# S5 inputs on TensorE: real and imaginary parts of two tiles in four row groups, with a swapped copy of the input

## The chip, the cores and the metric

One core of one Trainium2 chip runs the whole kernel. The metric is the device time of one launch in microseconds (us); less is better. TensorE (PE) multiplies, VectorE (DVE), ScalarE (ACT) and GpSimd (POOL) work elementwise, SyncE (SP) only issues DMAs. The engines run side by side, each in its own program order, and meet at semaphores.

## The reference, cut to what matters

A decoder block on x of 256 tokens by 2048 channels, float32. An RMSNorm and one wide projection `hn @ w_in` feed two token mixers, a Mamba-2 (SSD) mixer and an S5 mixer; their results are gated and merged, and a convolutional gated MLP follows. The change touches the S5 mixer alone:

```python
ug = u.reshape(b, seqlen, 64, 16)                     # 64 groups of 16 channels
bu = einsum("gpc,blgc->blgp", b_bar, ug)              # complex, 64 states a group
_, states = associative_scan(_lin_rec, (a_el, bu))    # over the 256 tokens
y = einsum("gcp,blgp->blgc", cmat, states).real + d_skip * ug
y = gelu(y); val, gate = split(y @ w_glu); return val * sigmoid(gate)
```

So for every group of 16 input channels, B (64 states by 16 channels, a real and an imaginary part) is multiplied with u over all tokens.

## The kernel before, in words

All activations lie channel-major: 128 channels on the partitions, the 256 tokens along the free axis. A large product is cut into units: 512 input by 256 output channels, 512 KB of weights. For each unit SP loads `raw` (L250) into a ring of 4 slots, ScalarE rounds it to a high half `whi` (L432), VectorE subtracts to get the low half `wlo` (L809), and TensorE runs 16 matmuls (L1363 on `whi`, 512 columns; L1365 on `wlo`, 256 columns). ScalarE reuses a slot only when TensorE has used it (`unit_used`). 588 units follow one another in the phases dt, u, zx, bc, gate, proj, glu, out, up and down.

In the phases zx (6 turns) and bc (2 turns) every turn has 16 units, four for each r of 0 to 3, and carries one block of the S5 mixer (blk 0 to 7): 8 groups of 16 channels, thus 128 input channels and 4 tiles of 128 states. Tile r takes the 32 input channels of rows 32r to 32r + 31. The steps of a block:

- `load_b` (L267 to 271, GpSimd DMAs) brings B into `bz`: rows 32r + 16g, both parts, block-diagonal; 8 DMAs a block.
- `ubs` is the block's 128 channels of u (`ub`). ScalarE makes the first (L593), GpSimd the later ones (L392), once the second drive of the block before is done.
- `s5_drive(blk, r)` (L1397 to 1408, TensorE) comes after the first unit of r = 0 and of r = 2 and computes tiles r and r + 1: 4 float32 matmuls of 32 rows by 128 columns on 256 tokens. The float32 matmuls appear in the trace as two records (passes) each. Tile r goes to PSUM bank 4 or 6, real part in the lower half and imaginary part in the upper half.
- VectorE turns the result back by the angle tables (`s5_turn_back` L956, `s5_inputs` L965), scans it (L976) and turns it on (L981, L982); `s5_products(blk)` (L1410 to 1420, TensorE), 16 float32 matmuls in four column groups, comes in the next turn and writes `YS5`, lower half of bank 5. `fill_c` (GpSimd, L380) prepares C for it.

GpSimd's order is written out by hand: constants, the loads of B for block 0, a long chain of small operations for the S5 parameters (L299 to L374, with the write of the decay rows, L354, in its midst) that ends in `cfold`, then `fill_c(0)`, then the loop over the blocks, then `load_decay` (L277) for the gate phase, which fills `dec` for VectorE's scan (L1104). VectorE copies the transposed time steps `DTT` (bank 5) to `dtt` at L1059, in the first turn, and TensorE waits for that in r = 1, q = 2 (L1433 and L1434).

A turn of VectorE has for every r: a `wlo`, the group's sums (L815), the turn back, a `wlo`, the causal convolution (L995), the scan, two further `wlo`, the turn on and the fractions of the angles (L953). In bc the convolution comes with every r, in zx with every second.

Of the kernel before, what the change touches and what calls it, by code (L numbers as in the profile page):

```python
# [24 lines left out]
F32, F32R, I32 = mybir.dt.float32, mybir.dt.float32r, mybir.dt.int32  # L25
ALU, ACTF = mybir.AluOpType, mybir.ActivationFunctionType
ds = bass.ds

P = 128
L = 256  # L30
# [64 lines left out]
def build_program(nc, a, out):  # L95
    ctx = ExitStack()
    with ctx:
# [4 lines left out]
        def at(name, shape, dt, off):  # L102
            size = 4 * math.prod(shape[1:])
            assert off + size <= room, (name, off, size, room)
            return nc.alloc_sbuf_tensor_at(name, shape, dt, offset=base + off)
# [14 lines left out]
        ub = at("ub", [P, 8, L], F32, 168 * K)  # L120
# [11 lines left out]
        bz = at("bz", [P, 2, P], F32, 138 * K)  # L132
        sx = at("sx", [P, 2, L], F32, 139 * K)
        ubs = at("ubs", [P, L], F32, 141 * K)
# [12 lines left out]
        W = 176 * K  # L147
# [7 lines left out]
        dtt = at("dtt", [P, 2, HEADS], F32, W + 20480)  # L155
        dtw = at("dtw", [P, 7, L], F32, W)
        ncz = at("ncz", [P, 4, 32], F32, W + 20864)

        C = W + 21 * K
        hw = at("hw", [P, 2, L], F32, 189 * K)  # L160
# [11 lines left out]
        scr = nc.dram_tensor("decay_rows", (HEADS, L), F32).ap()  # L172

        psum = ctx.enter_context(nc.psum_tensor("psum", [P, 8, 512], F32))
        BU = [psum[:, b, :].rearrange("p (c n) -> p c n", c=2) for b in (4, 6)]
        YS5 = psum[:, 5, 0:L]
        CB, XP = psum[:, 4, 0:ML], [psum[:, 5, 0:ML], psum[:, 6, 0:ML]]
        YY = [psum[:, 7, 0:L], psum[:, 7, L:2 * L], psum[:, 4, 0:L]]
# [1 line left out]
        DTT = psum[:, 5, 0:2 * HEADS].rearrange("p (s h) -> p s h", s=2)  # L180

        def sem(name):
# [3 lines left out]
        x_in, w_in, b_in = [[sem(f"{n}{k}") for k in range(4)] for n in ("x_in", "w_in", "b_in")]  # L186
# [13 lines left out]
        dtp_in, dt_in, dt_exp, dt_row, dt_T, dt_v = map(sem, ("dtp_in", "dt_in", "dt_exp", "dt_row", "dt_T", "dt_v"))  # L200

        s5_square, s5_inv, s5p_ready, u_ready, iota_ready, angm_ready = map(
            sem, ("s5_square", "s5_inv", "s5p_ready", "u_ready", "iota_ready", "angm_ready"))
        ubs_ready, ncz_ready, bu_used, modulus_ready = map(sem, ("ubs_ready", "ncz_ready", "bu_used", "modulus_ready"))
        th_ready, sincos, bu_ready, ang_ready, tab_ready, x5_ready, y5_ready, cz_ready, y5_out, y5_gelu, y5_hi, y5_lo = map(
            sem, ("th_ready", "sincos", "bu_ready", "ang_ready", "tab_ready", "x5_ready", "y5_ready", "cz_ready",
                  "y5_out", "y5_gelu", "y5_hi", "y5_lo"))
# [52 lines left out]
        def _(pool):  # L260
# [4 lines left out]

            def load_b(blk, r):

                for g in range(2):
                    pool.dma_start(bz[32 * r + 16 * g:32 * r + 16 * g + 16, :, 64 * g:64 * g + 64],
                                   a["s5_b"][ds(blk * 8 + (2 * r + g), 1), :, :, :]  # L270
                                   .rearrange("o c k n -> (o c) k n")).then_inc(b_in[r], 16)

            def load_decay(g, half):

                rows = scr[ds(g * HPG + half * HALF, HALF), :]
                for lo, off in ((0, 0), (P, L)):
                    pool.dma_start(dec[half][:, :, off:off + L - lo],  # L277
                                   rows[:, lo:L].rearrange("(o h) n -> o h n", o=1).to_broadcast([P, HALF, L - lo])
                                   ).then_inc(dec_in[half], 16)
# [96 lines left out]
            def fill_c(blk):  # L376

                for g in range(2):
# [2 lines left out]
                                  .rearrange("p c r n -> p r c n")).then_inc(cz_ready, 1)  # L381
                    pool.wait_ge(cz_ready, blk * 2 + (g + 1))

            pool.wait_ge(s5p_ready, 1)
            fill_c(0)
            pool.wait_ge(u_ready, 4)
            with pool.Fori(0, 7) as i:
                pool.wait_ge(bu_ready, i * 2 + 1)
                load_b(i + 1, 0)
                load_b(i + 1, 1)  # L390
                pool.wait_ge(bu_ready, i * 2 + 2)
                G.tensor_copy(ubs[:, :], ub[:, ds(i + 1, 1), :].rearrange("p o n -> p (o n)")).then_inc(ubs_ready, 1)  # L392
                load_b(i + 1, 2)
                load_b(i + 1, 3)
                pool.wait_ge(y5_ready, i + 1)
                fill_c(i + 1)
            pool.wait_ge(scr_w, 16)
            pool.wait_ge(dt_v, 1)
            load_decay(0, 0)
            pool.wait_ge(y5_ready, 8)  # L400
            load_decay(0, 1)
# [399 lines left out]
        def _(dve):  # L801
            step = Tally(dve, dve_step)
            V = nc.vector
# [146 lines left out]
            def s5_fractions(count):  # L950

                dve.wait_ge(angm_ready, count)
                V.scalar_tensor_tensor(ang[:, :, :], angm[:, :, :], MAGIC, ang[:, :, :], ALU.subtract,  # L953
                                       ALU.subtract).then_inc(ang_ready, 1)
# [85 lines left out]
            def mixer_turn(name, i, blk, prev):  # L1040

                _, per, quads, u0, g0 = phase(name)
                start = prev[0] == "u"
                for r in range(per):
                    def lo(j):
                        split_lo(u0 + r * quads + j + RING, i * (per * quads))
                    before = (name, i, r - 1) if r else prev
                    last = name == "bc" and i == 1 and r == per - 1
                    tile = blk * 4 + r
                    lo(0)  # L1050
                    group_sums(*before)
                    s5_turn_back(r, blk * 4 + (r + 1), blk * 2 + (r // 2 + 1), start and r == 0)
                    s5_inputs()
                    lo(1)
                    group_conv(*before)
                    if r == 0 and start:

                        dve.wait_ge(dt_T, 1)
                        V.tensor_copy(dtt[:, :, :], DTT).then_inc(dt_v, 1)  # L1059
                    if r == 1 and start:  # L1060
                        dve.wait_ge(scr_w, 16)
                    s5_scan(tile)
                    lo(2)
                    cpad_free(*before)
                    if r == 0 and not start:
                        s5_out(blk - 1)
                    s5_turn_on(r)
                    if not last:
                        s5_fractions(blk * 4 + (r + 2))
                    lo(3)  # L1070

            s5_fractions(1)
            dve.wait_ge(modulus_ready, 1)
            mixer_turn("zx", 0, 0, ("u", 0, 3))
            with dve.Fori(1, 6) as i:
# [266 lines left out]
        def _(pe):  # L1342
            mm = nc.tensor.matmul

            def unit(name, r, q, act, i=0):

                groups, quads, per = PHASES[name]
                n, g = UNIT0[name] + r * quads + q, GROUP0[name] + r
                pe.wait_ge(lo_ready, i * (per * quads) + (n + 1))
                if q == 0 and g + (i * per if isinstance(i, int) else 0) >= 2:  # L1350

                    pe.wait_ge(sum_ready, i * per + (g - 1))
                s, b = n % RING, 2 * (g % 2)
                for k in range(4):
                    row = 4 * q + k
                    x = act[:, row + (KT if name == "down" and row >= KT else 0), :]
                    first, last = q == 0 and k == 0, q == quads - 1 and k == 3
                    tiles = range(1 if name == "dt" else 2)

                    def cols(t):  # L1360
                        return slice(k * L + t * P, k * L + t * P + P)
                    for t in tiles:
                        mm(psum[:, b + t, :], whi[:, s, cols(t)], x, start=first, stop=False)  # L1363
                    for t in tiles:
                        ins = mm(psum[:, b + t, L:2 * L], wlo[:, s, cols(t)], x[:, 0:L], start=False, stop=last)  # L1365
                ins.then_inc(unit_used, 1)
# [7 lines left out]
            for k in range(KT):  # L1374
                c = k // 4
# [21 lines left out]
            def s5_drive(blk, r, first=False):  # L1397

                pe.wait_ge(ubs_ready, blk + 1)
                if not (first and r == 0):  # L1400
                    pe.wait_ge(bu_used, blk * 4 + r)
                for j in (r, r + 1):
                    pe.wait_ge(b_in[j], blk * 32 + 32)
                for k in range(2):
                    for j in (r, r + 1):
                        rows = slice(32 * j, 32 * j + 32)
                        ins = mm(BU[j % 2][:, k, :], bz[rows, k, :], ubs[rows, :], start=True, stop=True)
                ins.then_inc(bu_ready, 1)

            def s5_products(blk):  # L1410
# [11 lines left out]
            def mixer_turn(name, i, blk, prev):  # L1422

                for r in range(4):
                    for q in range(4):
                        if prev is None and r == 0:
                            pe.wait_ge(vlo_ready, q + 1)
                        unit(name, r, q, act16, i)
                        if q == 0 and r % 2 == 0:
                            s5_drive(blk, r, prev is None)  # L1430
                        if q == 1 and r == 0 and prev is not None:
                            s5_products(prev)
                        if prev is None and r == 1 and q == 2:  # L1433
                            pe.wait_ge(dt_v, 1)  # L1434

            mixer_turn("zx", 0, 0, None)
            with pe.Fori(1, 6) as i:
# [158 lines left out]
```

## Time and profile before

| | us |
|---|---|
| median of 3 runs (1750.8 to 1751.63) | 1751.62 |
| the profiled execution's own time | 1750.85 |
| its span, first to last instruction | 1749.2 |
| TensorE busy in the span | 1717.9 |
| VectorE busy | 1368.6 |
| ScalarE busy | 961.6 |
| GpSimd busy | 166.8 |

The mean granted TensorE clock is 0.998 of full speed. Busy times overlap between engines; TensorE's are modelled from pipelined matmuls, so that a busy TensorE need not be at its peak. The span is 1.65 us shorter than the execution's own time.

### The profile page before, as it was taken

To read this page: it belongs to the slowest core of one execution; us is meant where nothing else is said; L and a number is where in the kernel's file an instruction comes from. 1 tells how busy PE (TensorE), PEld (TensorE's weight loads), DVE (VectorE), ACT (ScalarE), POOL (GpSimd) and SP (SyncE) were. 2 spreads that over 40 slices of the span, in tenths; PEclk is the share of its full clock that TensorE was granted. 3 is DMA by queue.
4 is the path that set the end of the run, shared out by engine and by line. 5 is a ranking of instruction groups with operands and counts; after the bars stand their busy time and mean duration, and the time that the engine had idled before them with its cause. 6 is when DMAs were issued, how large, how long until landed. Compare 5 with 4: busy or idle time off the path is not lost.

```text
span 1749.2 us, 30494 instructions
## 1 busy us (share of the span) xinstructions
PE 1717.9 (98%) x10094; PEld 1483.0 (85%) x10094; DVE 1368.6 (78%) x1889; ACT 961.6 (55%) x1233; POOL 166.8 (10%) x240
## 2 busy tenths in 40 slices
PE   7999999999999999999999999999999999999997
PEld 6888888888788888888888888888888888888886
DVE  6999999999989898545886678888888888645544
ACT  6566666566656666645665554444444444444442
POOL 7920111101011110000001100000000000000000
PEclk9999999999999999999999999999999999999999
DMA  7555455545565655555566655555555555565652
GB/s 246 187 183 184 167 169 170 181 158 186 179 198 173 220 186 192 185 189 192 187 223 192 191 192 189 186 188 185 187 184 190 186 187 190 194 194 190 191 186 105
DMA packets 91415, 326.25 MB, mean 187 GB/s; under 512 B 11344, under 2 KB 12368, under 8 KB 91232
## 3 DMA queue, kind: packets, MB, share of 16 engines
q1 hardware_dynamic: 86320, 313.42, 54.3%
q0 software_dynamic: 5040, 12.11, 2.5%
q8 instruction: 32, 0.52, 0.1%
q14 instruction: 23, 0.19, 0.0%
HBM read 323.35 MB, written 2.15 MB: 186 GB/s over the span
## 4 chain that ended last, share of the span: by engine, by line
PE 62%; DVE 6%; issue 3%; ACT 2%; DVEq 1%; ACTq 0%
PE psum L1363 41%; PE psum L1365 20%; DVE dec L1104 2%; DVE wlo L809 1%; ACT whi L432 1%; ACT L444 1%; DVE zx L1162 0%; DVE zx L1165 0%; DVE gates L815 0%; DVE bc L995 0%; DVE zx L1085 0%; PE psum L1453 0%; DVE vn L1338 0%; DVE zx L827 0%; ACT rs L444 0%
## 5 line engine op out<-in xcount | busy, mean ns | idle before, releaser
L809 DVE TENSOR_TENSOR wlo<-raw,whi 128x1024 fp32r<-128x1024 f32 x588 | 720.5, 1230 | 321.2 <-ACT whi L432 319.6
L432 ACT ACTIVATE whi<-raw 128x1024 fp32r<-128x1024 f32 x588 | 619.1, 1057 | 442.3 <-PE psum L1365 433.5
L1363 PE MATMUL psum<-act,whi 128*128 128x512 f32 x1792 | 566.8, 398 | 0.0
L1363 PE MATMUL psum<-nw,whi 128*128 128x512 f32 x1552 | 488.7, 396 | 4.4 <-DVE wlo L809 4.2
L1365 PEld LDWEIGHTS psum<-act,wlo 128*128 128x128 f32 x1792 | 336.6, 188 | 79.6
L1365 PE MATMUL psum<-act,wlo 128*128 128x256 f32 x1792 | 352.2, 278 | 0.0
L1365 PEld LDWEIGHTS psum<-nw,wlo 128*128 128x128 f32 x1552 | 291.6, 188 | 68.2
L1365 PE MATMUL psum<-nw,wlo 128*128 128x256 f32 x1552 | 306.2, 278 | 0.0
L1363 PEld LDWEIGHTS psum<-act,whi 128*128 128x128 f32 x1792 | 272.7, 189 | 10.0 <-issue 6.6
L1363 PEld LDWEIGHTS psum<-nw,whi 128*128 128x128 f32 x1552 | 236.9, 189 | 6.4 <-issue 3.9
L1363 PE MATMUL psum<-ff,whi 128*128 128x512 f32 x704 | 221.1, 395 | 0.0
L1365 PEld LDWEIGHTS psum<-ff,wlo 128*128 128x128 f32 x704 | 132.2, 188 | 31.3
L1365 PE MATMUL psum<-ff,wlo 128*128 128x256 f32 x704 | 138.3, 278 | 0.0
L1363 PE MATMUL psum<-y_hl,whi 128*128 128x512 f32 x384 | 120.8, 396 | 0.0
L1363 PEld LDWEIGHTS psum<-ff,whi 128*128 128x128 f32 x704 | 107.2, 189 | 0.0
L760 ACT ACTIVATE tsum<-tsum 128x256 f32<-128x256 f32 x44 | 18.5, 419 | 131.2 <-DVE tsum L995 131.2
L1365 PEld LDWEIGHTS psum<-y_hl,wlo 128*128 128x128 f32 x384 | 72.1, 188 | 17.0
L440 ACT ACTIVATE hsum<-psum 128x512 f32<-128x512 f32 (+1 forms) x137 | 79.1, 577 | 10.0 <-PE psum L1365 10.0
L1363 PE MATMUL psum<-yb_hl,whi 128*128 128x512 f32 x256 | 80.4, 395 | 0.0
L1365 PE MATMUL psum<-y_hl,wlo 128*128 128x256 f32 x384 | 75.4, 278 | 0.0
L995 DVE SCALAR_TENSOR_TENSOR tsum<-cpad,parm,tsum 128x256 f32<-128x256 f32 x176 | 73.5, 480 | 0.1
L1363 PEld LDWEIGHTS psum<-y_hl,whi 128*128 128x128 f32 x384 | 58.5, 189 | 0.1
(186 smaller groups left out, 1389.0 us busy)
## 6 DMA issues: line engine op xcount, KB each, us to landing
raw<-in_w_up SPq DMA_DIRECT2D x176, 512.0 KB, 4.3
raw<-in_w_zx SPq DMA_DIRECT2D x96, 512.0 KB, 3.3
raw<-in_w_down SPq DMA_DIRECT2D x88, 512.0 KB, 4.2
raw<-in_w_gate SPq DMA_DIRECT2D x64, 512.0 KB, 3.8
raw<-in_w_proj SPq DMA_DIRECT2D x48, 512.0 KB, 3.3
raw<-in_w_bc SPq DMA_DIRECT2D x32, 512.0 KB, 3.2
raw<-in_w_glu SPq DMA_DIRECT2D x32, 512.0 KB, 3.2
raw<-in_w_out SPq DMA_DIRECT2D x32, 512.0 KB, 4.0
```

The lines of the kernel that those rows point to most:

```text
L432: fn(whi[:, s, :], raw[:, s, :], ACTF.Copy).then_inc(hi_ready, 1)
L440: fn(hsum[:, tiles, :], sums(g, 1)[:, tiles, :], ACTF.Copy).then_inc(hsum_ready, 1)
L444: step.done(fn(rs[:, :], NS, ACTF.Ln, bias=EPS, scale=1.0 / count))
L760: fn(tsum[:, 0, :], tsum[:, 0, :], ACTF.Silu).then_inc(silu2_done, 1)
L809: V.tensor_tensor(wlo[:, s, :], raw[:, s, :], whi[:, s, :], ALU.subtract).then_inc(lo_ready, 1)
L995: ins = V.scalar_tensor_tensor(to[t], src, col(w, q * taps + k), to[t], ALU.mult, ALU.add)
L1104: ins = V.tensor_tensor_scan(dec[half][:, k, :], dec[half][:, k, :], mask[:, :], 0.0, ALU.add, ALU.mult)
L1363: mm(psum[:, b + t, :], whi[:, s, cols(t)], x, start=first, stop=False)
L1365: ins = mm(psum[:, b + t, L:2 * L], wlo[:, s, cols(t)], x[:, 0:L], start=False, stop=last)
```

## The change

B's imaginary part is loaded 64 rows away from its real part (row group r ^ 2), from the same input. A second copy of u, `ubx`, has its halves of 64 rows swapped, so that these channels stand there too. The drive multiplies the real parts of tiles r and r + 1 in row groups r and r + 1, and the imaginary parts in the two others. Every one of the four products has a PSUM bank of its own: tile 0 or 2 in the lower halves of banks 6 and 7, tile 1 or 3 in the upper halves of banks 4 and 5. `load_b` issues 16 DMAs a block instead of 8, of half the size; `swap_u` issues 2 more. `ubx` lies where `dtw` and `dec` lie at other times, so `load_decay(0, 0)` waits for the last drive. The copy of `DTT` out of bank 5 moves ahead of the first turn, and TensorE's wait for it ahead of the first drive.

```diff
+        ubx = at("ubx", [P, L], F32, W)
...
-        BU = [psum[:, b, :].rearrange("p (c n) -> p c n", c=2) for b in (4, 6)]
+        BU = [psum[:, 6:8, 0:L], psum[:, 4:6, L:2 * L]]
...
             def load_b(blk, r):
 
-                for g in range(2):
-                    pool.dma_start(bz[32 * r + 16 * g:32 * r + 16 * g + 16, :, 64 * g:64 * g + 64],
-                                   a["s5_b"][ds(blk * 8 + (2 * r + g), 1), :, :, :]
-                                   .rearrange("o c k n -> (o c) k n")).then_inc(b_in[r], 16)
+                for k, at_r in ((0, r), (1, r ^ 2)):
+                    for g in range(2):
+                        row = 32 * at_r + 16 * g
+                        pool.dma_start(bz[row:row + 16, k, 64 * g:64 * g + 64],
+                                       a["s5_b"][ds(blk * 8 + (2 * r + g), 1), :, k, :]
+                                       .rearrange("o c n -> (o c) n")).then_inc(b_in[r], 16)
+
+            def swap_u(blk):
+
+                for to, frm in ((0, 64), (64, 0)):
+                    pool.dma_start(ubx[to:to + 64, :], ub[frm:frm + 64, ds(blk, 1), :]
+                                   .rearrange("p o n -> p (o n)")).then_inc(ubx_in, 16)
...
+            pool.wait_ge(u_ready, 1)
+            swap_u(0)
             pool.wait_ge(s5p_ready, 1)
             fill_c(0)
             pool.wait_ge(u_ready, 4)
...
                 pool.wait_ge(bu_ready, i * 2 + 2)
                 G.tensor_copy(ubs[:, :], ub[:, ds(i + 1, 1), :].rearrange("p o n -> p (o n)")).then_inc(ubs_ready, 1)
+                swap_u(i + 1)
                 load_b(i + 1, 2)
...
             pool.wait_ge(dt_v, 1)
+            pool.wait_ge(bu_ready, 16)
             load_decay(0, 0)
...
-                    if r == 0 and start:
-
-                        dve.wait_ge(dt_T, 1)
-                        V.tensor_copy(dtt[:, :, :], DTT).then_inc(dt_v, 1)
...
             s5_fractions(1)
+            dve.wait_ge(dt_T, 1)
+            V.tensor_copy(dtt[:, :, :], DTT).then_inc(dt_v, 1)
             dve.wait_ge(modulus_ready, 1)
...
                 for j in (r, r + 1):
-                    pe.wait_ge(b_in[j], blk * 32 + 32)
-                for k in range(2):
+                    pe.wait_ge(b_in[j], blk * 64 + 64)
+                pe.wait_ge(ubx_in, blk * 32 + 32)
+                for k, u in enumerate((ubs, ubx)):
                     for j in (r, r + 1):
-                        rows = slice(32 * j, 32 * j + 32)
-                        ins = mm(BU[j % 2][:, k, :], bz[rows, k, :], ubs[rows, :], start=True, stop=True)
+                        rows = slice(32 * (j ^ 2 * k), 32 * (j ^ 2 * k) + 32)
+                        ins = mm(BU[j % 2][:, k, :], bz[rows, k, :], u[rows, :], start=True, stop=True)
...
                         unit(name, r, q, act16, i)
+                        if prev is None and r == 0 and q == 0:
+                            pe.wait_ge(dt_v, 1)
                         if q == 0 and r % 2 == 0:
                             s5_drive(blk, r, prev is None)
...
-                        if prev is None and r == 1 and q == 2:
-                            pe.wait_ge(dt_v, 1)
```

## Rows read from the trace of the kernel before

**Rows 1.** Busy time, share of the span and instructions of each engine.

```profile
PE 1717.9 (98%) x10094; PEld 1483.0 (85%) x10094; DVE 1368.6 (78%) x1889; ACT 961.6 (55%) x1233; POOL 166.8 (10%) x240
```

**Rows 2.** Waits (us, times, longest): VectorE 123-369; timeline 380-394; TensorE's waits 386-492.

```profile
DVE wlo L809 <- ACT whi L432: 12.9, 23, 1.0
...
383.10 1.23 DVE L809 TENSOR_TENSOR wlo<-raw,whi 128x1024 fp32r<-128x1024 f32 x1 [1.01 <-ACT whi L432]
...
PE psum L1469 <- DVE ub L1004: 2.3, 1, 2.3
```

**Rows 3.** TensorE timeline (start, us) at two drives; the drive's line as a whole.

```profile
74.40 1.13 PE L1407 MATMUL psum<-ubs,bz 32*128 32x256 f32 x8
75.47 0.73 PE L1363 MATMUL psum<-act,whi 128*128 128x512 f32 x2
...
367.37 1.13 PE L1407 MATMUL psum<-ubs,bz 32*128 32x256 f32 x8
...
L1407 PE MATMUL psum<-ubs,bz x128: 374/374/478, 74.4 to 442.9; 32*128 32x256 f32 x128
```

**Rows 4.** TensorE timeline: full-array float32 passes, and the S5 products.

```profile
12.75 2.54 PE L1378 MATMUL psum<-xsq,ones 128*128 128x256 f32 x11
...
174.75 1.50 PE L1419 MATMUL psum<-st,cz 128*32 128x256 f32 x24
176.07 0.61 PE L1419 MATMUL psum<-st,ncz 128*32 128x256 f32 x8
```

**Rows 5.** GpSimd timeline: the end of the S5 parameters.

```profile
17.40 4.71 POOL L316 CAST iota<-iotai 128x256 f32<-128x256 int32 x1 [7.14 <-DMA craw<-in_s_c]
...
71.66 0.63 POOL L354 DMA_DIRECT2D decay_rows<-dtw  x1 [0.29 <-POOL s5p L309]
...
77.91 2.32 POOL L309 TENSOR_TENSOR ctmp<-craw,s5p 128x512 f32<-128x512 f32 x2
...
81.76 3.39 POOL L309 TENSOR_TENSOR ctmp<-craw,s5p 128x512 f32<-128x512 f32 x2
...
87.07 1.85 POOL L374 TENSOR_TENSOR cfold<-ctmp 128x512 f32<-128x512 f32 x1
```

**Rows 6.** VectorE timeline around the first drive.

```profile
74.80 0.73 DVE L953 SCALAR_TENSOR_TENSOR ang<-angm,ang 128x512 f32<-128x512 f32 x1
...
80.44 2.32 DVE L809 TENSOR_TENSOR wlo<-raw,whi 128x1024 fp32r<-128x1024 f32 x1
```

**Rows 7.** GpSimd's DMAs: landing of `bz` (L269), and issues with KB and landing.

```profile
DMA to landing us min/median/max: 1.7/2.7/3.8
...
decay_rows<-dtw POOLq DMA_DIRECT2D x1, 48.0 KB, 2.1
...
dec<-decay_rows POOLq DMA_DIRECT2D x16, 192.0 KB, 6.4
```

**Rows 8.** Stretches: length, busy (x) PE PEld DVE ACT POOL, PEclk, DMA, GB/s; PE timeline.

```profile
6.40:9.90 3.50, 3.50 (x8) 2.83 (x9) 2.54 (x6) 2.00 (x2) 3.17 (x9) 1.00 1.02 370
9.90:13.30 3.40, 3.40 (x17) 2.94 (x16) 3.40 (x9) 3.09 (x4) 0.36 (x2) 1.00 1.02 413
...
1737.59 1.13 PE L1520 MATMUL psum<-sq,ones 128*128 128x256 f32 x4 [2.00 <-ACT sq L749]
...
1740.80:1749.00 8.20, 0.00 (x0) 0.00 (x0) 4.63 (x4) 0.16 (x1) 0.00 (x0) 0.50 0.64 256
```

**Rows 9.** GpSimd and VectorE timelines in the mixer phase, and the first decay scan.

```profile
197.63 1.37 POOL L392 COPY ubs<-ub 128x256 f32 x1 [16.44 <-PE psum L1407]
198.94 2.00 POOL L269 DMA_DIRECT2D bz<-in_s_b  x4
...
198.66 0.68 DVE L815 TENSOR_TENSOR cpad<-psum,hsum 128x512 f32<-128x512 f32 x1
199.26 0.68 DVE L962 TENSOR_TENSOR rot<-psum,tab 128x512 f32<-128x512 f32 x1
...
471.98 2.64 DVE L1104 TENSOR_TENSOR_SCAN dec<-dec,mask 128x384 f32<-128x384 f32 x3
```

More of the change, by code:

```diff
@@ L203, in build_program @@
             sem, ("s5_square", "s5_inv", "s5p_ready", "u_ready", "iota_ready", "angm_ready"))
-        ubs_ready, ncz_ready, bu_used, modulus_ready = map(sem, ("ubs_ready", "ncz_ready", "bu_used", "modulus_ready"))
+        ubs_ready, ncz_ready, bu_used, modulus_ready, ubx_in = map(
+            sem, ("ubs_ready", "ncz_ready", "bu_used", "modulus_ready", "ubx_in"))
         th_ready, sincos, bu_ready, ang_ready, tab_ready, x5_ready, y5_ready, cz_ready, y5_out, y5_gelu, y5_hi, y5_lo = map(
```

## The prediction

> **What bounds the kernel now.** I read the busy times, then the waits, and last the order of time at the edited places. TensorE is busy 98% of the span [rows 1]. Over five turns of the Mamba/S5 mixer phase VectorE waits 12.9 us in 23 pieces [rows 2], always for the high halves that ScalarE makes, and those wait for TensorE to free a slot: 2.6 us of idle in a turn, in a stretch of 246 us that is five turns of 49.2. So TensorE sets the pace there. That ends at 383.10, VectorE's last wait [rows 2]. From 386 to 492 us VectorE waits for nothing (the view of its waits is empty), and TensorE in turn waits for it, 2.3 us in one piece [rows 2]. Two prices follow. A microsecond that TensorE loses before 383 us is a microsecond of the whole, since every weight unit behind it comes through a ring of four. A microsecond that it saves counts only before 383 us; one saved later is waited away.
>
> **What four row groups save.** A drive is 8 records: 4 float32 matmuls, each in two passes. Before, the first drive runs from 74.40 to the next unit's start at 75.47, 1.07 us; all 16 have the same record lengths [rows 3]. How long is one slot of 256 columns? Eleven full-array passes take 2.54 us, at most 0.231 each [rows 4]. The S5 products, in four column groups, put 24 passes between 174.75 and 176.07; four at a time that is 6 slots of 0.22 [rows 4]. So the drive now has 4 slots of 0.22 (two row groups side by side, re after im) and 0.19 of filling and draining. Four row groups with a bank each would leave 2 slots: 1.07 - 0.44 = 0.63. No row shows four row groups; bounds are no overlap beyond two (0 saved) and the four-wide pattern of the products (0.44 saved). I take 0.44, since the products show four-wide column groups at work and the drives show two row groups. Thirteen of the 16 drives start before 383 us (the 13th at 367.37 [rows 3]). 13 x 0.44 = 5.7 us saved; all 16 would be 7.0.
>
> **What the first swapped copy costs.** This is the largest term. Before, the first drive needs only `ubs`, made by ScalarE, and runs at 74.40 [rows 3]. Now TensorE also waits for `ubx`, and `swap_u(0)` stands on GpSimd behind its whole S5 parameter arithmetic. GpSimd finishes the last of it, `cfold`, at 87.07 + 1.85 = 88.92 [rows 5]. TensorE is an in-order engine: behind the waiting drive are all units of the phase; VectorE and ScalarE may only fill the ring, then stop.
> When does the copy land? VectorE will be idle from about 78 us, and the two engines slow each other: the pair of 128x512 products at 77.91 takes 1.16 each, the same pair at 81.76 takes 1.70 each, and beside them VectorE's 1.2 us subtraction takes 2.32 [rows 5, 6]. If the seven operations from 77.91 on all take 1.16 and 0.09 between them, they end at 77.91 + 7 x 1.16 + 6 x 0.09 = 86.6; at the latest at 88.9 as before. The issue: 0.3 us ahead, as before the write of the decay rows, and 0.6 for the first of two transfers (0.50 to 0.63 [rows 5, 9]). Landing: no row has an SBUF-to-SBUF transfer; `bz` lands in 1.7 to 3.8 us, the 48 KB write of decay rows in 2.1 [rows 7]; I take 2.1, the nearest in row length. 86.6 + 0.3 + 0.6 + 2.1 = 89.6, a stall of 15.2 us. Bounds: 86.6 + 0.5 + 1.7 = 88.8 (14.4) and 88.9 + 0.3 + 0.6 + 3.8 = 93.6 (19.2).
> The Trainium skill, "SBUF — State Buffer", explains that VectorE and GpSimd share one port pair by an exclusive lock; the pairs above agree. The skill's "DMA: Bandwidth & Descriptors", Anatomy of one DMA, gives 2.0 us plus the bytes at 436 GB/s for a GpSimd transfer, an estimate of 2.15 us for these 64 KB; with it the stall would be the same.
>
> **What the idle costs in clock.** At the kernel's start TensorE does 8 records in 3.50 us, then 17 of the same kind in 3.40 [rows 8]: for the first 3.5 us after idling it goes at half pace, that of the 1.2 GHz level, though the clock column, which has no entry so early, prints 1.00. At the end, its last record over by 1737.59 + 1.13 = 1738.7, it is granted 0.50, the lower level, from before 1740.8 [rows 8]. A stall of 15 us must bring that back: 3.5 us at half speed lose 1.7. Bounds: 0 if the clock stays, 3.5 if it needs twice as long.
> The Trainium skill, "TensorE: Matmul & The Clock Gate", Part 1, says that idling halves the clock and sustained work restores it; had I left the rule and these rows out, the sum would be 1.7 lower.
>
> **The rest, at nothing.**
> - GpSimd's DMAs. At the start 8 more issues of 0.5 us are 4 us, inside GpSimd's 7.14 us of idle before 17.40 [rows 5]. In a turn 8 more loads and 2 copies are 5 us; the copy goes out behind the drive of r = 2 and is wanted by the next r = 0 drive, about half a turn or 24 us later, of which the `ubs` copy ahead of it takes 1.37 [rows 9], the two issues 1 and the landing 2.1. If that cover were gone TensorE would wait for it once a turn. The issues don't slow VectorE: beside four of them at 198.94 its operations take the same 0.68 as elsewhere [rows 9].
> - VectorE reading two banks: it does so now in `add_halves`, 0.68 us for 128x512 at 198.66, the same as the rotation's 0.68 from one bank at 199.26 [rows 9].
> - The move of `dtt`. VectorE makes the copy (0.24 us) after 74.80 + 0.7 [rows 6], so about 75.7; `dt_T` is long there. TensorE now waits for it ahead of the first drive, 1.4 us behind where it would start. That lies inside the stall; without the stall it costs 1.4 us. It no longer waits in r = 1.
> - `load_decay(0, 0)` now waits for the last drive, which is over by 444 us (last record started 442.9 [rows 3]); its two issues and 6.4 us to land [rows 7] make it about 452; the scan wants it at 471.98 [rows 9]. Behind it on GpSimd is only the second half, which waits for the products of the last turn anyway.
>
> **Sum.** The profiled execution took 1750.85 us. +15.2 + 1.7 - 5.7 = +11.2, so 1762.1. The median of the runs, 1751.62, is 0.77 above it: 1762.8.
>
> **Rivals.**
> 1. The four groups do not run together (the change doesn't do what it says): nothing saved, 1762.8 + 5.7 = 1768.5. For it: no row has four row groups. Against it: two run side by side, and four column groups do. 0.10.
> 2. Faster. The swapped copy isn't late, so no stall and no clock loss: 1751.6 - 5.7 = 1745.9. Its place is GpSimd's order: the copy would have to be issued before 71.5 us, so the arithmetic to end 15 us earlier, or the hardware to run the transfer ahead of it. Below a stall of 4 us the sign turns (4.0 + 1.7 = 5.7). Against it: each of these operations stands in order and in its own row. 0.03.
> 3. GpSimd's extra issues hold VectorE: ten of 0.5 us a turn are 5 us, against 2.6 - 0.9 = 1.7 us idle left, so 3.4 lost in each of 7 turns: 1762.8 + 24 = 1787. Against it, the 0.68 beside the issues. 0.03. The Trainium skill's "SBUF — State Buffer" warns of descriptor writing locked out by VectorE; as that delays GpSimd rather than VectorE, it would only use up the cover of some 19 us.
> 4. No measurable change, by the stall being shorter than any bound: 0.02.
>
> **How the numbers follow.** The forecast has 0.82. About 0.2%, 3.5 us, is what a measurement can tell from no change. The forecast's own bounds are 14.4 + 0 - 7.0 = +7.4 and 19.2 + 3.5 - 5.7 = +17.0: 1759 to 1768.6. Taking in rival 1 gives 1759 to 1769. Slower 0.95, same 0.02, faster 0.03.
>
> **What would show it.** Right: TensorE idle for about 15 us before the first drive, released by the landing of `ubx`; a granted clock of 0.5 beside it and matmuls at double pitch for some 3.5 us; in all later drives 8 records and 0.63 us to the next unit; turns of 48.3 us instead of 49.2; a TensorE wait near the end of the phase grown from 2.3 to about 3.6 us; GpSimd's `cfold` done near 86.6. Wrong: later drives waiting for `ubx` or `bz`; drives still of 1.07 us; or the first drive at 74.4, which would void the largest term.

## The result and the profile after

The changed kernel takes 1762.99 us (median of 6 runs, 1762.44 to 1763.46) against 1751.62 before (1750.80 to 1752.53): ratio 1.0064, 95% interval 1.0054 to 1.0073. It is slower by 11.4 us. The profiled execution took 1762.64 us with a span of 1761.0.

The span and the busy times of the changed kernel, as in [rows 1]:

```profile
span 1761.0 us, 30707 instructions
PE 1717.2 (98%) x10094; PEld 1482.2 (84%) x10094; DVE 1366.8 (78%) x1889; ACT 961.4 (55%) x1233; POOL 195.4 (11%) x320
```

TensorE's two longest waits of the mixer phase, from the view of the waits (us in total, times, longest):

```profile
PE psum L1420 <- DMA ubx<-ub: 11.8, 1, 11.8
...
PE psum L1482 <- DVE ub L1018: 2.6, 1, 2.6
```

No engine has more instructions, GpSimd excepted (80 more, all DMA issues). The time is in one wait. The timeline of TensorE at the first drive, as in [rows 3]:

```profile
88.91 0.80 PE L1420 MATMUL psum<-ubs,bz 32*128 32x256 f32 x2 [11.81 <-DMA ubx<-ub]
88.93 0.80 PE L1420 MATMUL psum<-ubx,bz 32*128 32x256 f32 x2
89.47 0.66 PE L1420 MATMUL psum<-ubs,bz 32*128 32x256 f32 x2
89.52 0.64 PE L1420 MATMUL psum<-ubx,bz 32*128 32x256 f32 x2
90.08 1.22 PE L1375 MATMUL psum<-act,whi 128*128 128x512 f32 x2
```

and GpSimd's timeline ahead of it, as in [rows 5]:

```profile
72.98 3.93 POOL L319 TENSOR_TENSOR ctmp<-craw,s5p 128x512 f32<-128x512 f32 x2
...
79.19 3.38 POOL L319 TENSOR_TENSOR ctmp<-craw,s5p 128x512 f32<-128x512 f32 x2
...
85.09 1.26 POOL L384 TENSOR_TENSOR cfold<-ctmp 128x512 f32<-128x512 f32 x1
86.30 1.15 POOL L280 DMA_DIRECT2D ubx<-ub  x2
```

The first copy goes out when `cfold` is done, at 86.3, its second transfer lands at 88.8 and TensorE starts at 88.9 instead of 74.4. The two transfers from issue to landing, in the view of that line from 80 to 90 us:

```profile
DMA to landing us min/median/max: 1.9/1.9/2.0
```

The pair of matmuls at 90.08 takes 1.22 us instead of 0.73: half clock. The stretches show it (columns as in [rows 8]):

```profile
81.10:94.80 13.70, 5.89 (x22) 4.59 (x23) 5.20 (x8) 0.63 (x1) 6.67 (x8) 0.50 0.20 61
94.80:100.00 5.20, 5.20 (x32) 4.53 (x32) 3.55 (x5) 3.55 (x5) 0.69 (x2) 1.00 0.22 66
```

The granted clock is 0.50 from 81.1 to 94.8 us, of which 5.9 us lie behind the start of the first drive. That is the 1.2 GHz level; TensorE had idled since 88.91 - 11.81 = 77.1. (It was at this level in two other stretches, 19.7 to 26.5 and 490.7 to 494.1 us, of which more below.) Two later drives, in the same view of TensorE:

```profile
163.05 0.48 PE L1420 MATMUL psum<-ubs,bz 32*128 32x256 f32 x2
163.06 0.48 PE L1420 MATMUL psum<-ubx,bz 32*128 32x256 f32 x2
163.37 0.38 PE L1420 MATMUL psum<-ubs,bz 32*128 32x256 f32 x2
163.38 0.38 PE L1420 MATMUL psum<-ubx,bz 32*128 32x256 f32 x2
163.69 0.73 PE L1375 MATMUL psum<-act,whi 128*128 128x512 f32 x2
...
211.38 0.48 PE L1420 MATMUL psum<-ubs,bz 32*128 32x256 f32 x2
```

Four records start together, four more 0.32 us later, and the next unit follows 0.64 us after the start, where it took 1.06 to 1.07. A turn, between these two drives of the same r, is 48.33 us (49.2 before).

The shift of the k-th matmul of the weight units (k from 0) against the kernel before, worked out from both traces as the start in the run less the start in the kernel before, in us, shows where each run gains and loses:

| k-th matmul, its start before | after | e3 | e4 | e6 | e9 | e11 | e2 | e7 |
|---|---|---|---|---|---|---|---|---|
| 0, 17.4 | +0.9 | 0.0 | +1.3 | +0.5 | +0.6 | +0.4 | +1.0 | +0.5 |
| 290, 72.0 | +2.6 | +0.2 | +2.5 | +1.9 | +1.2 | +1.1 | +2.8 | +0.6 |
| 320, 78.4 | +16.7 | +18.1 | +2.5 | +16.5 | +17.1 | +13.7 | +2.6 | +0.2 |
| 440, 100.5 | +16.3 | +18.1 | +2.5 | +16.1 | +18.4 | +13.3 | +2.2 | +0.6 |
| 2000, 399.7 | +11.3 | +18.1 | +2.5 | +12.0 | +13.3 | +8.2 | -2.9 | -4.5 |
| 2300, 456.6 | +10.4 | +18.1 | +2.5 | +12.0 | +12.5 | +7.4 | -3.7 | -5.3 |
| 2500, 503.2 | +11.7 | +18.1 | +2.5 | +11.5 | +13.8 | +8.7 | +0.2 | -4.0 |
| the last, 1734.4 | +11.7 | +18.1 | +2.5 | +11.6 | +13.8 | +8.7 | +0.2 | -4.0 |

In the changed kernel the loss is all there at 78.4 us; 0.42 us come back at every drive; and from 456.6 to 503.2 some 1.3 us are lost again, as much as the last three drives had saved (3 x 0.42).

### The profile page after: what moved, and what is told of

It reads as the page before. It is cut to its first block, busy times and chain, and to the rows that moved or that the text cites. A ratio compares the mean times of both kernels' runs of the same rounds, so it can differ in the third digit from the quotient of the medians.

```text
span 1761.0 us, 30707 instructions
## 1 busy us (share of the span) xinstructions
PE 1717.2 (98%) x10094; PEld 1482.2 (84%) x10094; DVE 1366.8 (78%) x1889; ACT 961.4 (55%) x1233; POOL 195.4 (11%) x320
## 3 DMA queue, kind: packets, MB, share of 16 engines
HBM read 323.35 MB, written 2.15 MB: 185 GB/s over the span
## 4 chain that ended last, share of the span: by engine, by line
PE 62%; DVE 6%; issue 3%; ACT 2%; DVEq 0%; ACTq 0%
PE psum L1375 41%; PE psum L1377 20%; DVE dec L1116 2%; DVE wlo L823 1%; ACT whi L446 1%; ACT L458 0%; DVE zx L1174 0%; DVE zx L1177 0%; DVE gates L829 0%; DVE bc L1009 0%; PE psum L1466 0%; DVE zx L1097 0%; DVE vn L1350 0%; DVE zx L841 0%; ACT rs L458 0%
## 5 line engine op out<-in xcount | busy, mean ns | idle before, releaser
L1375 PEld LDWEIGHTS psum<-act,whi 128*128 128x128 f32 x1792 | 273.9, 189 | 11.3 <-issue 7.3
L1377 PEld LDWEIGHTS psum<-y_hl,wlo 128*128 128x128 f32 x384 | 72.1, 188 | 17.1
L273 POOL DMA_DIRECT2D bz<-in_s_b x128 | 62.4, 489 | 28.0 <-DVE ub L915 11.2
```

The source lines that it names most:

```text
L273: pool.dma_start(bz[row:row + 16, k, 64 * g:64 * g + 64], a["s5_b"][ds(blk * 8 + (2 * r + g), 1), :, k, :] .rearrange("o c n -> (o c) n")) ...
```

## The experiments

Each ran beside the kernel before on its chip; medians of that kernel were 1751.7 to 1751.9 us.

**e3_wait_only: the wait without the four groups.** The kernel before (two row groups, loads of B whole, `DTT` copied where it was), with `ubx` made and waited for and not read. `load_decay(0, 0)` waits for the last drive as in the changed kernel.

```diff
+            pool.wait_ge(u_ready, 1)
+            swap_u(0)
             pool.wait_ge(s5p_ready, 1)
...
                 for j in (r, r + 1):
                     pe.wait_ge(b_in[j], blk * 32 + 32)
+                pe.wait_ge(ubx_in, blk * 32 + 32)
```

> The kernel before, with the swapped copies made and waited for but not read: two row groups as before, loads of B as before. Theory: it has the whole stall and clock loss and no saving, 1763.0 + 5.5 = 1768.5 us, drives of 1.06 us, a wait of 12 us or more ahead of the first. Rival (the wait is made by the moved copy of DTT or by the split loads): 1751.6 us.

Measured: 1768.31 us (ratio 1.0091, 1.0076 to 1.0107). TensorE's wait, from the view of its waits:

```profile
PE psum L1420 <- DMA ubx<-ub: 14.7, 1, 14.7
```

The wait alone, with its clock, costs 16.4 us. In the medians the changed kernel is 5.3 us faster than this one, where 13 x 0.42 = 5.5 was expected of four row groups. The two profiled executions differ by 6.4 us: 0.5 because the first copy landed later here (the drive starts at 89.41), 0.84 at the first drive, which ran at half clock in both (2.01 us here, 1.17 in the changed kernel), and 12 x 0.42 = 5.0 at the twelve drives behind it. In the table e3 stays at +18.1 from 78.4 us to the end; nothing later takes it back.

**e4_loads_only: the doubled loads without the rest.** The kernel before, each load of B as two DMAs.

```diff
-                for g in range(2):
-                    pool.dma_start(bz[32 * r + 16 * g:32 * r + 16 * g + 16, :, 64 * g:64 * g + 64],
+                for k in range(2):
+                    for g in range(2):
+                        row = 32 * r + 16 * g
+                        pool.dma_start(bz[row:row + 16, k, 64 * g:64 * g + 64],
...
-                    pe.wait_ge(b_in[j], blk * 32 + 32)
+                    pe.wait_ge(b_in[j], blk * 64 + 64)
```

> The kernel before, with each load of B split in two (16 DMAs a block instead of 8), nothing else. Theory: hidden, 1751.6 us within 0.5, TensorE's first drive at 74.4. Rival (the 2.7 us by which the changed kernel is late even ahead of its first drive, with the clock halved from 19.7 to 26.5 us, come from the eight further loads at the start): 1754 us, the first drive at 77.

Measured: 1752.40 us (1.0002, 0.9993 to 1.0011). No difference in the mixer phase: its shift stays at +2.5 from 72 us on. By 44 us the profiled execution is late by 2.5 us, though, and has the rival's first drive, at 76.9:

```profile
76.89 1.13 PE L1409 MATMUL psum<-ubs,bz 32*128 32x256 f32 x8
```

The median is up by only 0.5 us, inside the spread. So GpSimd's further issues of loads cost nothing after the start, and what they do at the start is not settled by this run. Its profile does settle that the halved clock at 19.7 us is not what makes the changed kernel late there: e4 has no such stretch and is +2.5 at 72.0 us, against +2.6.

**e1_copy_early: the first copy ahead of the sines.**

```diff
             pool.wait_ge(modulus_ready, 1)
+            pool.wait_ge(u_ready, 1)
+            swap_u(0)
 
             pool.wait_ge(sincos, 2)
...
-            pool.wait_ge(u_ready, 1)
-            swap_u(0)
             pool.wait_ge(s5p_ready, 1)
```

> The changed kernel, with the first swapped copy issued as soon as GpSimd has the modulus, before it waits for the sines, instead of behind cfold. My theory (the loss is the late first copy and the clock it costs): TensorE no longer waits for ubx, but 1.4 us for the copy of DTT, and the drives still save 13 x 0.42 = 5.5 us: 1751.6 + 1.4 - 5.5 = 1747.5 us, faster than both kernels. Rival (the loss lies in GpSimd's doubled DMA issues over the whole mixer phase): about 1763, as now.

Measured: 1751.47 us (0.9998, 0.9989 to 1.0007). The wait for `ubx` is gone, and with it 11.5 us. The rival falls. But 4 us of the expected gain are missing. The view of the waits names 2.7 us of them, and beside them the wait for the copy of `DTT` that was expected; the profiled execution is also late by 2.4 us at 72.0 us, like the changed kernel, where the expectation had nothing:

```profile
DVE dec L1116 <- DMA dec<-decay_rows: 2.7, 1, 2.7
...
PE psum L1420 <- DVE dtt L1084: 1.3, 1, 1.3
```

**e2_copy_early_dtt: also the copy of DTT earlier.**

```diff
             lo(15)
+            dve.wait_ge(dt_T, 1)
+            V.tensor_copy(dtt[:, :, :], DTT).then_inc(dt_v, 1)
             normed_lo(3)
```

> As e1, and VectorE copies DTT one step earlier, ahead of the last low half of the normed input. Theory: the 1.4 us wait for the copy of DTT goes too, 1746.1 us. Rival (that wait is covered by something else): the same as e1 within 0.3 us.

Measured: 1750.06 us (0.9989, 0.9980 to 0.9998). The 1.4 us went as expected (1751.47 - 1750.06); the same 4 us are missing. In the table e2 is 3.7 us ahead of the kernel before at 456.6 and 0.2 behind it at 503.2. That is the 1.3 us that the changed kernel loses there too, and 2.5 us in which VectorE waits for the second half of the decay rows. GpSimd may load that half only when the last block's products have read the S5 states that lie there, and VectorE, which follows closely, comes for it before it has landed. GpSimd issues the load 3.1 us behind the end of the products here (470.54, then 473.60), against 0.3 us in the kernel before, and these 2.7 us are more than the whole wait; why it comes late stays open (last section).

**e7_products_early: the last products one unit earlier.**

```diff
                     unit("gate", 0, 1, act16, i)
-                    unit("gate", 0, 2, act16, i)
                     s5_products(7)
+                    unit("gate", 0, 2, act16, i)
```

> As e2, and the last block's S5 products come one gate unit earlier, ahead of the load of the second half of the decay rows that waits for them. In e2 VectorE waited 2.5 us for that load. Theory (this wait took back most of what the drives saved): it goes, 1750.1 - 2.5 = 1747.6 us. Rival (the wait is only moved, to another of VectorE's waits in that turn): 1750.1.

Measured: 1748.58 us (0.9982, 0.9973 to 0.9991). The view of VectorE's waits from 380 to 500 us no longer has the decay rows. 1.5 us of the median went instead of 2.5; the table's last column keeps -4.0 to the end. It is faster than the kernel before by 3.3 us.

**e8_loads_spread: half of the first loads of B later.**

```diff
-            for r in range(4):
+            for r in range(2):
                 load_b(0, r)
...
             swap_u(0)
+            for r in range(2, 4):
+                load_b(0, r)
```

> As e7, and of the first block's 16 loads of B the 8 for tiles 2 and 3 are issued behind the first swapped copy instead of at the start. Theory (16 loads at the start disturb the first inputs: units 1 to 3 us later in every profile with them, the median 0.5 us up in e4): 0.5 to 2.5 us less than e7, the first unit at 17.5 instead of 18.5 us. Rival (that lateness is chance): the same as e7.

Measured: 1747.70 us (0.9977, 0.9968 to 0.9986), 0.9 less than e7, whose runs span 1746.63 to 1751.34. In the profiles the first unit starts at 17.4 us in the kernel before, in e3 and here, and 0.4 to 1.3 us later in the ten kernels with all 16 loads at the start, which points to the loads. But at 72.0 us e8 is +0.5 and e7 +0.6, and e10 below, which has all 16 loads, measures 1747.82 us. So the difference of 0.9 between the medians shows nothing about the loads, and what they cost in all stays open. In its profile VectorE waits for the decay rows again, 1.8 us.

Part of the lateness of the first unit can be read from the timelines of GpSimd and VectorE, and it is not the transfers. The eight further issues push GpSimd's constants back. In the kernel before:

```profile
5.85 0.33 POOL L283 MEMSET cz<- 128x256 f32 x1
...
11.72 1.13 DVE L833 TENSOR_SCALAR xin<-xin,parm 128x256 f32<-128x256 f32 x4
```

and in the changed kernel:

```profile
9.57 0.37 POOL L293 MEMSET cz<- 128x256 f32 x1
...
11.90 1.64 DVE L847 TENSOR_SCALAR xin<-xin,parm 128x256 f32<-128x256 f32 x4
```

The constants, which end with a mask, were made by 10.3 us; now they last until 15.2 us and run beside VectorE's scaling of the input, whose last two groups of four take 1.64 and 1.30 us instead of 1.13 and 1.12. All ten kernels with 16 loads at the start have them at 1.64 to 1.83 and 1.30 us, the kernel before, e3 and e8 at 1.12 to 1.14: 0.7 us ahead of the first unit.

**e6_repeat_late and e9_repeat_early: what TensorE's time is worth, and where.** Both are the changed kernel with some drives computed more than once (the same result written again).

```diff
-                            s5_drive(blk, r, prev is None)
+                            s5_drive(blk, r, prev is None, 2 if name == "bc" and r == 2 else 0)
```

> The changed kernel with the drives of r = 2 in blocks 6 and 7 computed three times over: 4 more slots of 0.21 us on TensorE after 383 us of the kernel before, 1.7 us in all. Theory (from there on VectorE sets the end of the phase): 1763.0 us within 0.5, the units of the mixer phase 1.7 us later at its end, the first gate units after it not later than in the changed kernel. Rival (TensorE bound throughout): 1764.7.

Measured: 1762.81 us, against 1762.99 of the changed kernel. The slots are 4 in each of the two drives, 8 in all. In the table e6 is 0.2 us ahead of the changed kernel at 100.5, 1.6 behind it at 456.6, and 0.2 ahead again at 503.2. The added slots ran and cost nothing. TensorE's wait for VectorE fell from 2.6 to 1.9 us:

```profile
PE psum L1483 <- DVE ub L1018: 1.9, 1, 1.9
```

For e9 the condition is `4 if prev is None and r == 2`.

> The changed kernel with the drive of r = 2 in block 0 computed five times over: 8 more slots of 0.21 us, 1.7 us of TensorE, before 383 us. Theory (TensorE bound there): 1764.7 us, every later unit 1.7 us later. Rival (VectorE or the ring hides it): 1763.0.

Measured: 1764.28 us (1762.71 to 1765.84), 1.3 more than the changed kernel. In the profile it is 0.3 behind that kernel at 78.4, 2.0 behind at 100.5 and 2.1 at the end, so 1.7 us are added at the repeat and kept. Its four runs spread over 3.1 us, so the price is read from the trace rather than from the median. Of the two repeats the early one is paid, the late one is free.

**e5_warm and e11_warm30: the clock.** The changed kernel, TensorE kept busy in its wait; their product is used by nobody.

```diff
+                        if prev is None and r == 0 and q == 0:
+                            pe.wait_ge(iota_ready, 1)
+                            for _ in range(25):
+                                mm(psum[:, 4, 0:L], ones[:, :], iota[:, :], start=True, stop=True)
```

> The changed kernel, with 25 float32 matmuls of constants into an unused half bank ahead of the first drive: 25 x 0.43 = 10.8 us of TensorE inside its wait of 11.8 us. Their product is used by nobody. Theory (beside the wait itself the idle costs the clock, some 6 us at half speed, 2.7 us): the clock stays at full speed, the first drive comes at the same 89 us, and the median falls by 2.7 to 1760.3 us. Rival (the clock costs nothing that is not hidden): 1763.0.

Measured: 1762.01 us, four runs at 1759.45, 1760.58, 1763.45 and 1763.47. Neither theory: in the profiled one (1763.45) TensorE still idled before the drive, and the clock fell just then. Its timeline of TensorE:

```profile
75.63 10.96 PE L1445 MATMUL psum<-iota,ones 128*128 128x256 f32 x50
89.51 0.80 PE L1420 MATMUL psum<-ubs,bz 32*128 32x256 f32 x2 [2.93 <-DMA ubx<-ub]
```

and the stretch that begins with the drive (columns as in [rows 8]):

```profile
89.40:96.20 6.80, 6.69 (x25) 5.26 (x26) 2.05 (x4) 0.00 (x0) 0.00 (x0) 0.52 0.00 0
```

Half clock for most of 6.8 us. So e11 has 30 matmuls.

> As e5, with 30 matmuls (12.9 us) instead of 25. In e5's profiled execution TensorE still idled 2.9 us ahead of the first drive and the clock fell to half for 6.8 us; its four runs lay at 1759.5, 1760.6, 1763.5 and 1763.5. Theory: with the last idle cut to about 1 us the clock stays at full speed and the median comes to 1763.0 - 2.9 = 1760.1 us, with the first drive still at 89 to 90 us. Rival (the clock is not what separates the runs of e5): 1762 us or a spread as in e5.

Measured: 1760.24 us (1759.61 to 1760.98; ratio 1.0050). The timeline of TensorE has the drive at 88.49, with no idle listed ahead of it:

```profile
75.44 13.12 PE L1445 MATMUL psum<-iota,ones 128*128 128x256 f32 x60
88.49 0.48 PE L1420 MATMUL psum<-ubs,bz 32*128 32x256 f32 x2
```

and the stretch behind it keeps the clock:

```profile
88.90:94.80 5.90, 5.90 (x40) 4.95 (x33) 3.46 (x6) 2.47 (x4) 0.00 (x0) 1.00 0.00 0
```

In these 5.9 us TensorE has 40 records; the changed kernel had 22 in a stretch with as much busy time. The clock's share is 1762.99 - 1760.24 = 2.75 us in the medians. In the profiles, right behind the stall (the row of 78.4 us in the table), e11 is +13.7 and the changed kernel +16.7, and 0.4 of that is the earlier start of e11's drive; that leaves 2.6 for the clock. The Trainium skill, "TensorE: Matmul & The Clock Gate", HAM oscillation, says that a gap in a kernel's matmuls is paid a second time as a cold start behind it; these runs agree, with 2.75 us behind 11.8.

**e10_shifted: GpSimd's late issue.** e7 with 24 empty instructions on GpSimd ahead of its wait for the S5 inputs.

```diff
+            for _ in range(24):
+                pool.nop(nofuse=True)
             pool.wait_ge(s5_in, 32)
```

> As e7, with 24 empty instructions on GpSimd in its idle time near the start. In the four kernels with the early swapped copy GpSimd issues the second half of the decay rows 3.0 us after the products that it waits for, in the six others 0.3 us. Theory A (it depends on where this instruction stands in GpSimd's stream): 0.3 us here. Theory B (on what VectorE holds at that moment, or on the waits): 3.0 us as in e7. Time as e7, 1748.6 us, in both.

Measured: 1747.82 us (0.9978, 0.9968 to 0.9988). The issue still comes 3.0 us after the products' end (467.97, then 471.02). Theory A as tried here falls; B is not shown by that. The median is 0.8 us below e7's, with nothing changed but the empty instructions: medians of such kernels differ by as much without a cause that is known.

## Why the prediction was right, point by point

- **The first copy.** Predicted: `cfold` done at 86.6, landing and start at 89.6, a stall of 15.2 us against the start at 74.4. Measured: `cfold` done at 86.35; the issue at once, not 0.3 us later; the second transfer issued at 86.92 and landed at 88.78, thus 1.9 us where 2.1 was taken from the write of the decay rows; the start at 88.91, thus 14.5. The term was 0.7 too large by these three small errors of the same sign. The wait that the profile names is 11.8, not 14.5: TensorE came to it 2.7 us later than before. That lateness is covered, because the copy lands by GpSimd's clock, not by TensorE's; e3 came early, waited 14.7 and started at 89.4. The Trainium skill, "DMA: Bandwidth & Descriptors", Anatomy of one DMA, gives an estimate of 2.15 us for such a transfer; the first two took 1.98 and 1.86 us, the median of all 16 is 2.6 (1.9 to 4.3).
- **The clock.** Predicted 1.7 us, from the 3.5 us at half pace at the kernel's start. Measured 2.75 (e11 by the medians; 2.6 by the profiles), since 5.9 us behind the stall ran at 1.2 GHz. This is the term that was sized wrong; it was bounded by 3.5. How long the slow stretch is differs from case to case here: 3.5, 5.9 and in e5 6.8 us.
- **Four row groups.** Predicted 0.44 a drive and 0.63 left; measured 0.42 and 0.64. 13 drives: 5.7 predicted, 5.3 by e3's median, 5.45 by 13 x 0.419 in the trace. Rival 1 falls.
- **Where a saving counts.** Predicted: before 383 us only, with TensorE's late waits growing from 2.3 to about 3.6. That 1.3 us saved late are waited away is so: the table gives them back from 456.6 to 503.2, VectorE waits for nothing from 397 to 503 us, and e6 and e9 show it by price: 8 late slots free, 8 early ones paid. TensorE's waits, which were to show it, grew by less than forecast. The wait that was 2.3 us is 2.6, and all of TensorE's waits in that stretch are 3.4 us against 3.1 before (2.3 and 0.8). In the changed kernel TensorE also ran at the lower clock level from 490.7 to 494.1 us and so took longer over its work. In e11, where it did not, the waits are 2.6, 0.8 and 0.8, thus 4.2, nearer to the forecast growth of 1.3; e11 loses the same 1.3 us between 456.6 and 503.2 (+7.4, then +8.7), so that late slow stretch cost nothing.
- **The sum.** 14.5 + 2.75 - 5.45 = 11.8, the difference of the spans (1761.0 - 1749.2). Predicted 11.2: 0.7 too much for the stall, 1.0 too little for the clock, 0.3 too much for the groups. Part of the agreement to 0.2 us in the median is these errors cancelling.
- **The rest at nothing.** The copy of `DTT` came at 81.6, not 75.7: VectorE was 2.7 us late ahead of it, and beside GpSimd's 128x512 products its last four operations took 7.9 us instead of 4.5; it lay inside the stall, and without the stall it cost the 1.4 us predicted (e1 against e2). GpSimd's issues in the turns cost nothing (the loads in e4, the copies in e3), so rival 3 falls; its sum had a slip, 3.4 for 3.3 us a turn. `load_decay(0, 0)` landed at 463.8 us, 10.4 of them the shift of that place, and nobody waited for it. At the start GpSimd's idle had room for the 8 further issues, as said; what they push back was not considered: GpSimd's constants now run beside VectorE's first operations, which lose 0.7 us by it ahead of the first unit (under e8). What of that and of the rest of the lateness at 72.0 us is left in the median stays open; e4's is up by 0.5, inside the spread.
- **Rival 2** was not far off in kind. Its 1745.9 left out the 1.4 us for `DTT` that the prediction itself puts on a kernel without the stall. With the copy early, it is missed by e1 (1751.5) for `DTT`, the decay rows and the start, and by e7, e8 and e10 (1748.6, 1747.7, 1747.8) for less. Once the first copy is in time the whole is 3 to 4 us faster than the kernel before. The table puts that gain at the drives, but no run gave the kernel before the two other moves of e7, so that they add nothing of their own is argued and not shown.

## What to carry to other kernels

When a change adds an input to a step, look first for the engine that makes it and where in that engine's order it stands: here a copy that takes 2.5 us from first issue to last landing cost 14.5 us because it was queued behind arithmetic that nobody on the critical path was waiting for. A stall of the engine that sets the pace can cost its clock too, 2.75 us here. And before a saving is counted, find the point from which another engine sets the time; there a doubled copy of the saved work shows at once whether it was worth anything.

## What the runs showed of the hardware that was not expected

- The clock also falls behind idles far shorter than the stall, and not every time. In e5 it fell behind 2.9 us of idle. Ahead of the first unit the changed kernel idles 3.25 us and e2 3.38, and the granted clock went to 0.50; e1 and e4 idle 3.25 and 3.26 there, and it stayed. In TensorE's wait for `ub` near the end of the mixer phase it fell behind 2.62 us (changed kernel), 2.34 (e4) and 1.87 (e6), and stayed behind 2.33 (before), 2.60 (e9) and 2.59 (e11). In the kernel before TensorE idles 2.0 us near its end without a fall [rows 8].
- One cause of the spread between runs of the same kernel may lie here. In e8 the six shortest of ten runs (1746.95 to 1748.00 us) have a mean clock of 0.996 to 0.998, the four others (1748.84 to 1749.72) 0.995 to 0.996; in e5 the two at 1759.45 and 1760.58 us have 0.996 and 0.998, the two at 1763.5 us 0.994. It wasn't tried.
- GpSimd's DMA issue behind a semaphore came 0.3 us after the last product in eight kernels and 3.0 to 3.1 us after it in the five with the early copy (e1, e2, e7, e8, e10). In those VectorE runs operations on SBUF operands at that moment; so it does in others. The Trainium skill, "SBUF — State Buffer", SBUF: two separate sides, has GpSimd's descriptor writing locked out by some VectorE operations; no run here isolates that, and 24 instructions of shift did not change it. The cause stays open, and VectorE's waits for the decay rows in e1, e2 and e8 hang on it in part.
- Four 32-row groups run as close together as four 32-column groups: records 7 ns apart, 0.42 us saved for two slots.
